# Hybrid S5 and sparse-attention decoder step on one core: another order of transposes, scores and values in the prompt attention

## What is computed

```python
def block(args):
    q_b, g_b, pos, i = args
    qf = q_b.astype(f32) * (HEAD_DIM ** -0.5)
    s_c = jnp.einsum('nqhgd,njhd->nhgqj', qf, kc)
    p_c = jax.nn.softmax(jnp.where(m_c, s_c, NEG_INF), axis=-1) * m_c
    o_c = jnp.einsum('nhgqj,njhd->nqhgd', p_c, vc)
    ...
    p_s = jax.nn.softmax(jnp.where(m_s, s_s, NEG_INF), axis=-1)
    o_s = jnp.einsum('nhgqkl,nhqkld->nqhgd', p_s, v_g)
    ...
    p_w = jax.nn.softmax(jnp.where(m_w, s_w, NEG_INF), axis=-1)
    o_w = jnp.einsum('nhgqk,nkhd->nqhgd', p_w, kw[:, :, 1])
    return g_b[..., 0:1] * o_c + g_b[..., 1:2] * o_s + g_b[..., 2:3] * o_w
```

## Time and profile before

| | before |
|---|---|
| median of 3 runs | 784.72 us (783.44 to 785.08) |
| profiled execution, its own time | 783.84 us |
| span of the profiled execution | 782.0 us |
| mean granted TensorE clock | 0.997 |
| PE busy | 753.1 us (96% of the span) |
| DVE busy | 380.0 us |
| ACT busy | 201.7 us |
| POOL busy | 101.2 us |

### The profile page before, as it was taken

How to read it: one execution, slowest core, us unless ns; L and a number is a source line. 1 busy time by engine, 2 the same in 40 slices (tenths; PEclk the granted TensorE clock), 3 DMA queues, 4 the chain that set the end, 5 groups by cost and what they waited for, 6 DMA issues and landing times.

```text
span 782.0 us, 13225 instructions
## 1 busy us (share of the span) xinstructions
PE 753.1 (96%) x5200; PEld 483.8 (62%) x5200; DVE 380.0 (49%) x853; ACT 201.7 (26%) x478; POOL 101.2 (13%) x154
## 2 busy tenths in 40 slices
PE   8999999999999999988999999999999999998995
PEld 5455588777778787655566774445656565553442
DVE  3279522997323224656645578435631211214866
ACT  3010212112223355455434100144111111123223
POOL 3000006000000011234520100011210110015002
PEclk9999999999999999999999999999999999999998
DMA  9640393750573359400011487013899999996002
GB/s 323 169 129 0 99 296 142 78 159 31 169 117 53 111 183 270 126 1 1 1 70 55 126 294 289 0 41 130 330 407 410 415 419 415 417 368 198 19 15 107
DMA packets 81160, 136.49 MB, mean 175 GB/s; under 512 B 33798, under 2 KB 57418, under 8 KB 76882
## 3 DMA queue, kind: packets, MB, share of 16 engines
q1 hardware_dynamic: 64572, 110.14, 42.5%
q0 software_dynamic: 3728, 13.38, 5.0%
q10 hardware_dynamic: 12798, 12.12, 4.6%
HBM read 116.52 MB, written 21.19 MB: 176 GB/s over the span
## 4 chain that ended last, share of the span: by engine, by line
PE 81%; DMA 9%; DVE 4%; ACT 3%; issue 1%; POOL 0%; SPq 0%; DVEq 0%; POOLq 0%; ACTq 0%
PE ps L1221 24%; PE ps L1313 10%; PE ps L1687 6%; PE ps L1935 6%; PE ps L1482 4%; PE ps L1819 4%; PE ps L1228 3%; PE ps L1807 3%; DMA merged<-in_w_exp_down 3%; DMA w_slot<-in_w_exp_down 3%; PE ps L1851 2%; PE ps L1568 2%; PE ps L1516 2%; PE ps L1549 2%; DMA wgu<-expert_rows,pos_i 1%
## 5 line engine op out<-in xcount | busy, mean ns | idle before, releaser
L1221 PE MATMUL ps<-w_slot,hT 128*128 128x396 f32 (+1 forms) x176 | 64.0, 523 | 0.3 <-DVE hT L2011 0.3
L1221 PE MATMUL ps<-hT,w_slot 128*128 128x288 f32 x256 | 63.1, 407 | 0.0
L1221 PEld LDWEIGHTS ps<-hT,w_slot 128*128 128x128 f32 x256 | 48.3, 190 | 13.9 <-issue 0.8
L3025 DVE SCALAR_TENSOR_TENSOR th<-th,ps 128x256 f32<-128x256 f32 x12 | 5.1, 421 | 102.9 <-ACT th L2281 102.9
L1221 PEld LDWEIGHTS ps<-w_slot,hT 128*128 128x128 f32 x176 | 33.1, 190 | 28.6 <-issue 10.0
L1819 PE MATMUL ps<-w_slot,hT 128*32 128x256 f32 x544 | 49.7, 380 | 0.0
L1313 PE MATMUL ps<-hT,w_slot 128*128 128x288 f32 x144 | 37.3, 407 | 0.0
L1482 PE MATMUL ps<-qg,w_slot 128*128 128x288 f32 x128 | 35.9, 414 | 0.0
L2762 DVE TENSOR_REDUCE nm_p<-ps 128x2 f32<-128x256 f32 (+3 forms) x32 | 24.9, 818 | 16.9 <-PE ps L1516 16.8
L1819 PEld LDWEIGHTS ps<-w_slot,hT 128*32 128x32 f32 x544 | 26.3, 110 | 10.0 <-issue 2.3
L1090 POOL TENSOR_TENSOR hT<-hT,w_p 128x512 f32<-128x512 f32 (+3 forms) x11 | 25.1, 2283 | 53.9 <-DVE w_p L2393 53.9
(11 more groups left out here) (515 smaller groups left out, 1395.6 us busy)
## 6 DMA issues: line engine op xcount, KB each, us to landing
w_slot<-in_w_in SPq DMA_DIRECT2D x10, 1024.0 KB, 8.6
merged<-in_w_exp_down SPq DMA_DIRECT2D x10, 1024.0 KB, 16.0
wgu<-in_w_exp_gate SPq DMA_DIRECT2D x8, 1024.0 KB, 13.5
wgu<-in_w_exp_up SPq DMA_DIRECT2D x8, 1024.0 KB, 15.6
w_slot<-in_w_exp_gate SPq DMA_DIRECT2D x8, 1024.0 KB, 12.9
w_slot<-in_w_exp_up SPq DMA_DIRECT2D x8, 1024.0 KB, 15.1
w_slot<-in_w_exp_down SPq DMA_DIRECT2D x6, 1024.0 KB, 14.3
expert_rows<-onsaT ACTq DMA_DIRECT2D x12, 512.0 KB, 8.5
```

The lines of the kernel that those rows point to most:

```text
L1221: ins = pe.matmul(out, a, b, start=(n == 0), stop=(n == len(pairs) - 1))
```

## The change

From unit 6 on the first two turns of a unit's group stand ahead of the unit's scores, and the values of the turns that were made before stand right behind the scores (`ready`). The second exponential `("e", i, 1)` now comes behind the next pair of turns and its values. Fillers 4, 5 and 6 stood in units 6, 8 and 12; now 4 stands in unit 8 and 5 in unit 10, both behind the values that follow the scores, and 6 stands at the end of unit 10 behind the compressed scores. These three are copied by DVE, and the alternation goes on behind each as if it had not been there, so ACT makes 30 copies and DVE 34 (before: 32 and 32). No instruction is added or removed, and none computes something else.

```diff
             3: [("kc", 0, 0), ("t", "ab", 1), ("cs", 0, 0)], 4: [("t", "ab", 2), ("vcp", 0, 0)], 5: [("vcs", 0, 0), ("t", "ab", 3)],
-            6: [("t", "ab", 4)], 8: [("t", "ab", 5)], 12: [("t", "ab", 6)], 17: [("t", "ab", 7)]}
+            17: [("t", "ab", 7)]}
+BEHIND_VALUES, BEHIND_UNIT, FIRST_HOISTED = {8: 4, 10: 5}, {10: 6}, 6
...
     for i in range(len(UNITS) + U_LAG):
+        turns = [(i - U_LAG, c) for c in unit_chunks(i - U_LAG)] if i >= U_LAG else []
+        if i in CACHED_AT:
+            turns = turns + [("cached", CACHED_AT[i] + j) for j in range(2)]
+        ready = []
+        if FIRST_HOISTED <= i < len(UNITS):
+            while len(waiting) < AT_ONCE:
+                waiting.append(turns.pop(0))
+            steps.extend(("t", v, c) for v, c in waiting)
+            ready, turned[:] = list(turned), waiting
+            waiting.clear()
         if i < len(UNITS):
             steps.append(("s", i, 0))
             steps.append(("e", i, 0))
+        for v, c in ready:
+            value(v, c)
+        if i in BEHIND_VALUES:
+            steps.append(("t", "ab", BEHIND_VALUES[i]))
         rest = [("e", i, 1)] if i < len(UNITS) else []
...
-        turns = [(i - U_LAG, c) for c in unit_chunks(i - U_LAG)] if i >= U_LAG else []
-        if i in CACHED_AT:
-            turns = turns + [("cached", CACHED_AT[i] + j) for j in range(2)]
...
         steps += rest
+        if i in BEHIND_UNIT:
+            steps.append(("t", "ab", BEHIND_UNIT[i]))
...
-        _e = "act" if len(TURN_OF) % 2 == 0 else "dve"
+        _e = "act" if (TURN_OF[_i, _c] - SHIFTED) % 2 else "dve"
+        if _i == "ab" and _c in BY_DVE:
+            _e, SHIFTED = "dve", SHIFTED + 1
```

More of the change, by code:

```diff
@@ L220 @@
 SLOT_OF, TURN_OF, VALUE_OF, TAKEN_BY = {}, {}, {}, {}
+BY_DVE, SHIFTED = list(BEHIND_VALUES.values()) + list(BEHIND_UNIT.values()), 0
 for _w, _i, _c in PROMPT:
```

## The result

The changed kernel takes 777.99 us (median of 6 executions, 777.5 to 779.42) against 784.9 for the kernel before in the same comparison; the ratio is 0.9924, 95% interval 0.9905 to 0.9943. One of the six executions of the kernel before took 981.56 us, far above all others, and is not in the ratio; without it their median is 784.72.

The account below looks back on a forecast made before the run. PE was taken to bound the kernel and the stage; 7.4 us of waits by the starts less 3.4 left afterwards gave a gain of 4.0, hence a median of 780.7 us, range 779.0 to 784.0.

Parts of the forecast that it names:

- 0.88 twice at the compressed scores: Units 6 and 14: only a pair of turns left behind the compressed scores before the next scores; 0.88 us lost each.
- the order on DVE: Units 9 and 15: weights ahead of a hoisted turn's copy make the turn two later 0.2 late each, 0.4 together.
- the tie: Second exponential against next scores, from unit 12: 6.10 us needed, 6.13 of PE work; 0.15 put for one late boundary.
- The products are the same, so the sum is waits that go less waits that stay or come: Whole stage: gain counted from PE's waits alone, 7.4 lost before less 3.4 afterwards, 4.0 us.
- 6.6 us: Stage from 325 to 407 us: PE busy 75.37 of 82.0, so only 6.6 us was said to be winnable.
- The median of the runs shown is 0.9 higher: Baseline: median 784.72 against 783.84 profiled; the same offset took the changed kernel from 779.8 to a forecast 780.7.
- The other way of copying them is under 0.1 and hidden: Fillers copied by DVE instead of ACT: effect under 0.1 us, hidden, since nothing PE needs is queued then.
- the wait of 0.97: One of ten PE waits before: a turn behind a filler whose copy can begin only at the filler's end.
- B: Rival: second exponentials 0.5 late at five boundaries, units 10/11 to 14/15, giving back 2.5: 783.2 us; chance 0.14.
- D: Rival: copies waiting for turns hold exponentials, scores and next turns at nine boundaries, 6.3 comes back: 787.0 us; chance 0.05.
- C: Rival: stage's gain absorbed later, where a stream with transfers in the chain feeds the experts: 784.7 us; chance 0.08.
- E: Rival: unit 15, DVE's product of compressed probabilities and mask waits up to 3.6 for POOL's scaling: 782.5 us; chance 0.03.

Follow-up runs that it names:

- the kernel with the compressed scores ahead: Changed kernel, but from unit 6 second exponential and compressed scores stand between a unit's second turns and their values: 775.35 us, ratio to before 0.9886.
- the second profile of before: The kernel before, unchanged, run again for another profile: median 785.89 us, ratio 1.0021 to the kernel before.
- the fillers only: Changed kernel without hoisted turns, keeping the new places and copiers of fillers 4, 5 and 6: 778.49 us, ratio to before 0.9921.

## Why the prediction was right and wrong

- **The waits were right.** It had 7.4 lost before by the starts and 3.4 afterwards. By the same count, in the same places, the profile after has 0.94, 0.95, 0.51 and 0.52 at the four shown waits and about 0.5 in small ones (0.23 behind filler 6, 0.18 in unit 9, 0.07 in unit 15): 3.4. It said 0.88 twice at the compressed scores, 0.46 twice behind fillers, 0.15 behind filler 6, 0.4 for the order on DVE and 0.15 for the tie, so single terms were up to 0.15 off and cancelled: that they add up to 3.4 to the tenth is luck. The gain of 4.0 by the waits that it named is there.
- **"The products are the same, so the sum is waits that go less waits that stay or come" failed.** This is the step that makes the stage's gain too small, 4.0 where it is 5.58. Two things are missing in it. First, the order changes what a product's neighbours let it take: a pair of turns ahead of a mask is some 0.1 shorter, 0.93 in all, while the compressed scores ahead of turns take 0.94 and 0.95 where they took 0.84 and 0.86, 0.19 in all. Second, two waits of before were inside merged rows and not in the list of waits. A row like this one, of the kernel before in unit 6, takes 1.30 to the next start where eight transposes take 1.02; the second half waits for the copy of the filler ahead of it, and unit 12 has it again:

```profile
326.64 1.37 PE L1549 MATMUL ps<-ident,hT 128*128 128x128 f32 x8
327.94 0.65 PE L1568 MATMUL ps<-work,kv 128*64 128x256 f32 x4
```

  That is 0.56, and the four values at 350.20 hide 0.16 more (0.74 to the next start instead of 0.58). So the waits give 4.0 + 0.56 + 0.16 = 4.7 and the neighbours 0.93 - 0.19 = 0.74, together 5.5 of the stage's 5.58. Nor is "6.6 us" of idle "all that lies there": the kernel with the compressed scores ahead has a stage 7.66 shorter than before.
- **The baseline was mis-sized, as far as the runs tell.** "The median of the runs shown is 0.9 higher" was taken as an offset that both kernels have. It isn't: the changed kernel's median is 0.4 above its profiled execution. Of 58 executions of before 41 have a mean clock of 0.995 or less, and their median is 1.7 above that of the others; of the changed kernel's 6 one has. From 783.3, the median of the executions of before with 0.996 or more, to 777.99 it is 5.3, the stage's gain; the remaining 1.5 up to its overall median would be mostly the clock. That share is argued, since only profiled executions show where the clock went. That a wait could cost more than its length was in no rival.
- **"The other way of copying them is under 0.1 and hidden" failed.** With the turns hoisted it is worth 0.46 of stage, without the hoist 2.0. And the wait of 0.97 was misread as one for a copy that "can begin only at the filler's end": the copy stood behind four exponentials on ACT and began 1.1 later. The forecast had credited the turns' waits to the hoist; the fillers and the copiers remove nearly as many without it. The waits' sum was right for the whole change and its attribution was wrong.
- **The tie in units 12 to 14 held.** No mask of units 8 to 14 waited for a second exponential; B and D did not happen. ACT after, unit 13: the exponentials, with a short copy between them, are done at 375.20, and unit 14's mask began at 375.38.

```profile
372.24 0.69 ACT L2200 ACTIVATE hT<-ps,nm_p 128x512 f32<-128x512 f32 x1 [2.01 <-DVE nm_p L2779]
...
374.97 0.23 ACT L2200 ACTIVATION_READ_ACCUMULATOR hT<-ps,nm_p 128x1 f32 x1
```

- **C and E did not happen.** The loads moved by 5.4 and 5.3. DVE's product of the compressed probabilities with their mask in unit 15 ran at 388.60, 1.43 behind the end of POOL's scaling (387.17), and took 0.42 as before; it met none. In the tail one more 0.8 came in the profiled pair: the wait for the experts' last gather was 2.66 in the one execution and 1.76 and 0.29 in the other. It is 2.09 in the second profile of before and lies between 0.83 and 2.47 in the ten other kernels (2.47 with the fillers only), so part of it is chance; how much belongs to the change is open.

## What to carry to other kernels

Where the bounding engine has short waits, add them by the starts of its instructions and look into merged rows too, and ask what each product takes next to its new neighbour. Then read the mean clock of every execution, not of the profiled one alone: here a cluster of waits, 2.3 us in all, cost 1.64 more in lost clock in one profile and nothing in another, and moving one filler there brought 2.05 of median where its waits alone were put at 1.1. In a pipeline of turns and copies, try who copies before moving the work: handing the first copy, and the filler's, to the engine that is free sooner removed 1.8 us of shown waits (1.5 by the starts) without moving a product, and on top of the new places it took 2.0 off the stage.

## What was not expected of the hardware

- PE's granted clock fell to 1.2 GHz though PE never stood still for more than 1.1 us in this stage: in the second profile of the kernel before it had been busy for 1.77 of the 4.00 us ahead, in waits of 0.72, 0.51 and 1.08. With the same waits in the first profile it stayed at 2.4 GHz. It was low for 3.4 us at a time, in one case 6.8, and 3.4 us of it cost 1.64 (86.08 against 84.44). TensorE: Matmul & The Clock Gate (the Trainium skill, What's actually happening) has the throttled clock as the default that activity releases, and a monitor that is not in step with the kernel; that the same waits lose the clock in one execution and keep it in another agrees with that.
- Eight transposes take 0.96 to 1.03 to the next start ahead of a chunk's values (weights 128x64) and 0.87 to 0.93 ahead of a mask (128x128).
